# SSD stage: ScalarE makes one tap and the bias of each convolved tile, VectorE the other three taps

## What is computed

```python
z, xbc, dt_raw, q, k, v, g_ssd, g_att = split_cols(u @ w_in.astype(u.dtype), IN_WIDTHS)
xbc = jax.nn.silu(causal_dwconv(xbc, conv_w, conv_b))      
xs, bm, cm = split_cols(xbc, (SSD_INNER, SSD_GROUPS * SSD_STATE, SSD_GROUPS * SSD_STATE))
dt = jax.nn.softplus(dt_raw.astype(f32) + dt_bias.astype(f32)) * valid_f32[None, :, None]
...
y = ssd_chunked(xh, dt, a, bm.reshape(bsz, lp, SSD_GROUPS, SSD_STATE),
                cm.reshape(bsz, lp, SSD_GROUPS, SSD_STATE))
```

## Time and profile before

| | |
|---|---|
| runs shown (3) | 2597.35 us median, 2590.88 to 2600.04 |
| profiled execution | 2598.12 us, its span 2596.3 us |
| busy over the span | PE 2459.7 (95%), DVE 1554.5 (60%), ACT 881.1 (34%), POOL 62.5 (2%) |
| the chain that ended last | PE 83%, DVE 7%, issue 5%, ACT 3% |
| SSD stage, both passes | about 1387 to 1843 us of the span; steps 0 to 12 of the first pass end at about 1480, those of the second at about 1714 |
| mean PEclk | 0.972 |

### The profile page before, as it was taken

The page is one execution under the profiler, slowest core; times in us unless marked ns, Lnnn a source line. Parts: engine busy times, 40 slices in busy tenths (PEclk is TensorE's granted clock), DMA queues, the critical chain, the costliest instruction groups (busy, mean ns, idle before and its releaser), DMA issues.

```text
span 2596.3 us, 39893 instructions
## 1 busy us (share of the span) xinstructions
PE 2459.7 (95%) x15333; PEld 2185.1 (84%) x15333; DVE 1554.5 (60%) x2793; ACT 881.1 (34%) x1347; POOL 62.5 (2%) x55
## 2 busy tenths in 40 slices
PE   7999999999989899999998989988998999999998
PEld 4887888878778888888888879888997999999997
DVE  5555344446467765344467876776665655883784
ACT  3122222234345433222244762574322333222222
POOL 0000000000112000000000000000100000000000
PEclk9999999999989899999998999998999999999999
DMA  4236222344442002222223422441221122223223
GB/s 144 87 102 127 97 97 97 105 152 113 137 121 68 27 18 92 97 98 94 85 96 108 110 63 83 115 98 49 93 86 63 63 82 82 83 95 129 83 85 110
DMA packets 91773, 242.48 MB, mean 93 GB/s; under 512 B 24886, under 2 KB 58166, under 8 KB 67638
## 3 DMA queue, kind: packets, MB, share of 16 engines
q1 hardware_dynamic: 29056, 198.26, 21.8%
q10 hardware_dynamic: 60808, 36.42, 6.6%
q0 software_dynamic: 1760, 5.77, 1.0%
HBM read 230.51 MB, written 11.14 MB: 93 GB/s over the span
## 4 chain that ended last, share of the span: by engine, by line
PE 83%; DVE 7%; issue 5%; ACT 3%; ACTq 1%; DMA 1%; DVEq 0%
PE ps L958 40%; PE ps L1190 27%; PE ps L1291 3%; PE ps L1144 3%; PE ps L1089 1%; PE ps L1127 1%; DVE wlo L1451 1%; PE ps L1376 1%; ACT whi L516 1%; ACTq L616 1%; PE ps L1350 1%; ACT L L803 1%; DMA buckets<-in_buckets 1%; PE ps L975 1%; PE ps L1048 1%
## 5 line engine op out<-in xcount | busy, mean ns | idle before, releaser
L516 ACT ACTIVATE whi<-raw 128x2048 fp32r<-128x2048 f32 x187 | 357.7, 1913 | 752.0 <-PE ps L958 510.9
L1190 PE MATMUL ps<-parts,whi 128*128 128x264 f32 x2752 | 484.5, 293 | 11.0 <-DVE sq L2072 5.6
L1451 DVE TENSOR_TENSOR wlo<-raw,whi 128x2048 fp32r<-128x2048 f32 (+1 forms) x197 | 431.5, 2191 | 67.9 <-ACT whi L516 67.3
L958 PE MATMUL ps<-parts,whi 128*128 128x512 f32 x1360 | 433.0, 400 | 4.8 <-DVE parts L1668 4.8
L1190 PEld LDWEIGHTS ps<-parts,whi 128*128 128x128 f32 x2752 | 392.1, 191 | 23.4 <-issue 17.8
L958 PEld LDWEIGHTS ps<-parts,whi 128*128 128x128 f32 x1360 | 258.0, 190 | 68.2 <-issue 7.2
L958 PE MATMUL ps<-parts,wlo 128*128 128x512 f32 x680 | 270.7, 398 | 0.0
L1190 PE MATMUL ps<-parts,wlo 128*128 128x264 f32 x1200 | 245.0, 286 | 0.0
L958 PE MATMUL ps<-Mhi,whi 128*128 128x512 f32 x512 | 204.0, 398 | 4.7 <-DVE Mlo L1542 4.7
L958 PE MATMUL ps<-Mlo,whi 128*128 128x512 f32 x512 | 203.7, 398 | 0.0
L958 PE MATMUL ps<-Mhi,wlo 128*128 128x512 f32 x512 | 203.6, 398 | 0.0
(11 more groups left out here) (361 smaller groups left out, 3880.6 us busy)
## 6 DMA issues: line engine op xcount, KB each, us to landing
raw<-in_stream SPq DMA_DIRECT2D x187, 1024.0 KB, 4.8
bands<-scratch ACTq DMA_DIRECT2D x8, 1024.0 KB
csb<-sums_d ACTq DMA_DIRECT2D x16, 512.0 KB, 5.7
near<-bands ACTq DMA_DIRECT2D x20, 256.0 KB, 2.7
csf<-sums_d ACTq DMA_DIRECT2D x32, 128.0 KB, 6.0
Qst<-parts POOLq DMA_DIRECT2D x14, 256.0 KB, 6.1
tabs<-bands ACTq DMA_DIRECT2D x8, 418.0 KB, 4.2
X<-in_x SPq DMA_DIRECT2D x4, 512.0 KB, 14.9
```

What stands on the lines that cost most here:

```text
L516: nc.scalar.activation(whi[:, s, :], raw[:, s, :], ACT.Copy).then_inc(hi_done, 1)
L958: mm = nc.tensor.matmul(out, w[:, s, at], x(k), start=k + j == 0, stop=k == k_tiles - 1 and j == 2)
L1190: mm = nc.tensor.matmul(ps[:, 2 * par + h, 0:HALF], w[:, s, at], x[:, k, h * HALF:(h + 1) * HALF], start=k + j == 0, stop=k == k_tiles - 1 ...
L1451: low = nc.vector.tensor_tensor(wlo[:, s, a:b], raw[:, s, a:b], whi[:, s, a:b].bitcast(F32), ALU.subtract)
```

## The change

In steps 1 to 12, ACT now makes last tap and bias of tile r-1 as one Identity activation (scale and bias are columns of `hv`) once DVE has evacuated the tile (`mt_free`), and gives `tap_new`. DVE waits for `tap_new` and makes the other three taps. The activation stands behind `next_unit`, behind the DMA issues of step 5, and behind `decays(0)` in step 6; it stands ahead of the scan's part of the step and of the Silu.

```diff
@@ ACT
+                    if 0 < r <= 12:
+                        act.wait_ge(mt_free, i * 28 + (T0["half"] + r))
+                        nc.scalar.activation(conv_out(r - 1), stg[:, (r - 1) % 2, SSD_TAPS - 1:], ACT.Identity,
+                                             scale=conv_vec(r - 1, 3), bias=conv_vec(r - 1, 4)).then_inc(tap_new, 1)
                     if r in SCAN_AT:
@@ DVE
-            with own.loop(2, 89) as i:
+            with own.loop(2, 77) as i:
...
                     dve.wait_ge(mt_free, i * 28 + (T0["half"] + r + 1))
                     to, x = conv_out(r), stg[:, r % 2, :]
-                    own.mark(nc.vector.tensor_scalar(to, x[:, 3:3 + TOK], conv_vec(r, 3), conv_vec(r, 4), ALU.mult, ALU.add))
+                    dve.wait_ge(tap_new, i * 12 + (r + 1))
                     for tap in range(3):
-                        own.wait()
+                        if tap:
+                            own.wait()
                         last = nc.vector.scalar_tensor_tensor(to, x[:, tap:tap + TOK], conv_vec(r, tap), to, ALU.mult, ALU.add)
```

More of the change, by code:

```diff
@@ L346, in program @@
         tokh_ready, xbc_new, xs_ready = sem("tokh_ready"), sem("xbc_new"), sem("xs_ready")
+        tap_new = sem("tap_new")
         cs_loaded = [sem("cs_loaded0"), sem("cs_loaded1")]
```

## The result

The changed kernel took 2615.59 us (median of 7 runs, 2610.30 to 2619.03) beside 2595.81 us for the kernel before (7 runs); the ratio is 1.0068, 95% interval 1.0054 to 1.0081. The ratio is an estimate from all the runs and not the quotient of the two medians; by the medians the difference is 19.8 us. On a second chip it took 2613.87 us beside 2599.58, ratio 1.0062 (1.0048 to 1.0075). The forecast was 2612 us, range 2603 to 2619, and slower. The profiled execution took 2615.8 us, its span 2614.0 (before 2596.3). DVE was busy for 1542.8 us (1554.5 before), ACT for 902.6 (881.1), PE for 2463.5 (2459.7).

What follows compares the result with a forecast made beforehand. PE sets the pace, with ACT's own queue the path in steps 5 and 6. First pass 9.3 - 1.65 + 1.3, second 3.9 - 1.65 + 1.3 + 2.5: +15.0 us, forecast 2612 us, range 2603 to 2619.

Steps and rivals of the forecast that it cites:

- Prices: Operation lengths assumed: ACT tap 0.80 us (0.65 to 0.90), DVE's three taps 2.38, table load 1.28, tap end to Silu 2.46.
- Second pass, steps 5 and 6: +3.9: Tap behind ACT's DMA issues, then DVE's taps, delay the Silu; PE's turn in step 7 comes 3.9 us later.
- First pass, steps 1 to 6: +9.3: DVE enters late without slack: 5.4 us of backlog by step 4, 3.9 from steps 5 and 6, at PE's turn.
- The rival without the backlog: DVE catches up in the first pass, both passes pay alike: +3.5 us, 2601, no change that can be told; chance 0.14.
- the sign given for it: Profile sign for the first pass: PE's wait for ACT's Silu at step 7 grows from 3.6 to 10 to 11 us.
- Steps 7 to 12: -1.65 a pass: DVE has one operation less before the scan, so PE's waits in steps 9 to 11 shrink: -1.65 us a pass.
- neither bound: Bounds for steps 7 to 12: 0 if ACT falls behind in steps 8 and 10, -2.84 if all waits go.
- Step 12 into 13: +1.3 a pass: Tap behind the high part delays DVE's taps; PE's wait of 2.06 us in step 14 grows 1.3 in both passes.
- Clock: +2.5 in the second pass: After about 7 us of waiting at step 7, PE drops to the lower clock: +2.5 us; first pass paid already.
- The sum: Whole kernel: first pass 8.95 us, second pass 6.05, together +15.0 us, 0.57% slower.
- DVE as the limit: Rival: DVE's 14.2 us of lost work is all on the path, time 2583, faster; chance 0.04.
- The longer table switch: Rival: a switch holds ACT 2.46 us, hidden under DVE's work after the change; 4.7 us less, 2607.5; chance 0.04.

Runs made afterwards that it cites:

- this part alone: ACT makes the tap in steps 5 and 6 only, DVE all four taps elsewhere, against the kernel before: 2606.77 us, ratio 1.0022.
- Alone, steps 1 to 4: ACT makes the tap in steps 1 to 4 only, DVE all four taps elsewhere, against the kernel before: 2607.00 us, ratio 1.0018.
- 1.30 alone: ACT makes the tap in step 12 only, DVE all four taps elsewhere, against the kernel before: 2606.16 us, ratio 1.0017.
- the kernel with the tap first: Changed kernel with ACT's tap moved to the head of its step; against the kernel before: 2603.06 us, ratio 1.0012.
- PE filler: Changed kernel plus 48 unread matmuls ahead of PE's wait for the Silu in step 7; against the kernel before: 2615.39 us, ratio 1.0065.
- less work for DVE alone (steps 7 to 11): ACT makes the tap in steps 7 to 11 only, DVE all four taps elsewhere, against the kernel before: 2603.93 us, ratio 1.0007.
- three moved lines: Kernel before, all taps on DVE, with step 6's Silu issued ahead of the decays; against the kernel before: 2588.81 us, ratio 0.9961.

## Why the prediction was right, and where not

**Prices.** The tap takes 0.82 us, 0.80 was taken. The table load lies wholly under DVE's three taps, and tap end to Silu is 2.44 us (1671.60 to 1674.04), 2.46 was taken. Right.

**Second pass, steps 5 and 6: +3.9.** Z-T grew by 3.83 and 4.31 us, and by 4.33 with this part alone. Right to within 0.5 us. From ACT's exponential of the sums to PE's turn all three take 18.1 to 18.3 us, against 13.9 in both profiles of before, so the part itself cost 4.2 to 4.4; ACT's six DMA issues account for 0.2 to 0.4 of the excess (4.39 to 4.56 us in all, 4.17 and 4.23 before). In the profile that shows 3.83 the stretch from Z to that exponential was 0.6 us shorter than before, and why is not shown.

**First pass, steps 1 to 6: +9.3.** Measured 9.28 and 9.29 (S-T of the first two profiles, and of the second two). Alone, steps 1 to 4 gave 5.20 (5.4 said) and steps 5 and 6 3.83 (3.9). The exponential of the sums moved from 1408.17 to 1413.69, 5.4 after the shift of the start. Right. The rival without the backlog is out. The path was right too, but the sign given for it was not: PE waits 8.89 us at this turn, where "10 to 11" was said. The prediction counted 2.4 us of waiting for the token copy and no clock; some 1.6 us more passed in the low clock behind that wait.

**Steps 7 to 12: -1.65 a pass.** The stretch 9-11 gave 0.85 to 1.17, T-9 gave 0.58 where the clock was full in both kernels (23.36 to 22.78). Together 1.4 to 1.75. The size is right, and neither bound holds. The waits that were to show it shrank less than said: 1.06 and 0.77 us in step 9, 1.20 and 0.88 in step 11, where 0.6 was said; the one in step 10 went, as predicted.

**Step 12 into 13: +1.3 a pass.** Measured 1.22 in the whole, 1.30 alone. The size is right and the way was told only in half. Behind the taps DVE's mask of step 13 (`cbm`) is late, then ACT's copy of B, its decays and DMA issues, and the Silu of z; DVE then stood idle for 5.12 us (4.04 before) ahead of the gating until that Silu was done. Up to `cbm` the 1.3 us travel through DVE's queue, as said; from there they travel through ACT's:

```profile
1490.56 0.27 ACT L840 ACTIVATE Btok<-ps 16x128 f32<-16x128 f32 x1 [2.84 <-DVE cbm L1933]
...
1498.55 0.65 ACT L850 ACTIVATE stg<-stg 128x528 f32<-128x528 f32 x1
```

```profile
1499.23 0.71 DVE L1971 TENSOR_TENSOR Y<-Y,stg 128x528 f32<-128x528 f32 x1 [5.12 <-ACT stg L850]
```

**Clock: +2.5 in the second pass.** This step failed, though the pair of traces seems to bear it out (T-9 grew by 2.12). The premise "with a wait of some 7 us the second pass will drop too" holds; but "after 3.12 us the mean stayed 1.00" was one execution, and the kernel before pays 26.10 us there in another. Against that one the changed kernel is 0.6 to 0.9 us shorter, and some 0.6 of this is the tap's own gain, which the sum counts elsewhere: the kernel with the tap first, whose clock falls only at the end of a wait of 3.90 us, also reads 25.47 there. With that taken off the term lies between -0.3 and +2.7, by which execution of before one takes; against the PE filler's turn at full clock, in the changed kernel itself, it is 0.7 to 1.0. For the first pass the prediction had "paid already", that is 0. There T-9 fell by 1.4 to 1.5 (25.85 and 25.93 to 24.48 and 24.46), 0.6 of it the tap's and 0.8 the clock's: the clock fell while PE still waited and was back about 3 us behind the turn, where before it took 5 to 6. The unedited 14-Z, which was only in the bounds, read higher in its place: the two passes together took 159.8 and 159.7 us against 156.9 and 157.6. That is no loss that can be told from scatter. Without a longer wait at step 14 the sum of the two 14-Z reads 155.6 to 160.9 over the kernels of the table, with a wait of 3.1 us 158.3 to 159.8.

**The sum.** +15.0 was said; +17.7 and +16.1 measured by the ratios, +13.6 to +17.3 by the stage sums of two profiles each. Without 14-Z the stage sums give +11.3 to +14.5. So the stretches that were reasoned out come to 0.5 to 3.7 us less than was said, and which it is depends on the execution of before, through its clock. That the ratios read 1 to 3 us more than was said comes from stretches outside of the reasoning, such as 14-Z; that the total met the forecast so closely is in part luck.

**The rivals.** DVE as the limit: out, since less work for DVE alone (steps 7 to 11) gave no time that a run can tell. The longer table switch: in the loads that nothing covers, the next ACTIVATE still starts 1.29 to 1.30 us after the load's start (1653.20 to 1654.50, and 1661.40 to 1662.70, above). The Trainium skill, "ScalarE: Activation LUTs", section "What ACT_TABLE_LOAD costs", has a drain of some 1.38 us on top; none of these loads shows it, and the measurement decides. The same section prices an ACTIVATE at 186 ns and 0.833 ns a column with some 93 ns for each pointer operand, 0.81 us for this tap (an estimate from its figures); the trace agrees with 0.82.

## What to carry to other kernels

Moving work to the engine with a third of its time busy was a loss here because that engine does its instructions in order (the tap began only behind the high part, the DMA issues and the decays) and stood on the path in just those steps. Ask where in the other engine's queue the new instruction stands, and what must come back before that queue goes on: the same 24 activations cost 16 us behind the step's other work and 3 us ahead of it. The same reading pays without the change: the instruction that the bottleneck waits for goes ahead of those that have slack, which gave 10 us for three moved lines. And take a second profile of the kernel before: a term of 2.5 us was read here from one, and the next did not show it.

## What was not expected of the hardware

- The granted clock behind an idle spell of PE of about 3 us is not fixed by its length: 1.00 after 3.12 and 3.14 us, 0.50 after 2.97 and 3.19 us, in the same place of the program. Behind all the turns that waited 3.45 us or longer, up to 8.89, it was at 0.50 within 2 us, behind the one that waited 1.67 us it stayed 1.00. At other places it fell behind less (0.50 behind the 2.36 us of step 4 in the changed kernel) and stayed 1.00 behind as much (3.14 us at step 14 of the second pass in its second profile).
- One DMA issue on ACT can take three times as long as its like (1.95 us against 0.62) with nothing changed in its queue ahead of it, and what stands behind it on ACT is late by as much (the Silu by 1.3 us). Why is not shown.
